# Moving SBUF operands of a three-block network to other byte offsets

## The reference

```python
x = first_block(x, c, positions, ...)    # 2 layers: swiglu, hybrid conv/MLA or NSA attention, swiglu
x = second_block(x, mem, ...)            # 2 layers: forgetting attention + feed-forward, conv + mixture of 8 experts
return third_block(x, mem, ...)          # pooled + MoBA attention, cross attention, conv feed-forward

def swiglu(h, w13, w2):
    a, b = jnp.split(h @ w13, 2, axis=-1)
    return (jax.nn.silu(a) * b) @ w2
```

## The kernel before, in words

| operand | address before | offset before |
|---|---|---|
| `hh`, `hl` | 24736, 32928 | 160 |
| `whi`, `wlo` | 86400, 119168 | 128 |
| `AR` | 179488 | 32 |
| `f_gh`, `f_gl` (float 224 of `AR` and on) | 180384 | 160 |
| `uh`, row k (float 3840 + 264 k) | 194848 + 1056 k | 32, 64, 96, 128, 160, 192, 224, 0 |
| `e_zeh`, `e_zel`, `e_gh`, `e_gl` | 182560 and on | 32 |

## Time and profile before

### The profile page before, as it was taken

The page is one execution under the profiler, slowest core; times in us unless marked ns, Lnnn a source line. Parts: engine busy times, 40 slices in busy tenths (PEclk is TensorE's granted clock), DMA queues, the critical chain, the costliest instruction groups (busy, mean ns, idle before and its releaser), DMA issues.

```text
span 3083.6 us, 48420 instructions
## 1 busy us (share of the span) xinstructions
PE 2999.6 (97%) x20659; PEld 2751.1 (89%) x20659; DVE 2343.1 (76%) x2704; ACT 1725.0 (56%) x1982; POOL 73.7 (2%) x143
## 2 busy tenths in 40 slices
PE   9999999999989999899989999999999999999999
PEld 8999899999979998899987888888888888899999
DVE  6887788888657566665777898898898898766675
ACT  5435443534535445444655777777777777555553
POOL 0110001010000000000000000000000000000000
PEclk9999999999999999999999999999999999999999
DMA  8785468587513543255415998998999899533353
GB/s 335 283 317 195 163 245 302 212 308 258 199 69 142 215 162 138 76 192 191 148 64 209 364 358 334 365 355 333 365 356 366 333 359 366 213 124 137 123 201 114
DMA packets 112381, 739.27 MB, mean 240 GB/s; under 512 B 12480, under 2 KB 12480, under 8 KB 32160
## 3 DMA queue, kind: packets, MB, share of 16 engines
q1 hardware_dynamic: 92304, 662.77, 57.3%
q0 software_dynamic: 19856, 73.34, 6.8%
HBM read 735.01 MB, written 1.05 MB: 239 GB/s over the span
## 4 chain that ended last, share of the span: by engine, by line
PE 86%; DVE 9%; ACT 3%; issue 1%; DMA 0%; SPq 0%; DVEq 0%; ACTq 0%
PE ps L560 65%; PE ps L559 19%; PE ps L569 2%; DVE wlo L2983 2%; ACT whi L1986 2%; DVE AF L2962 1%; DVE att L2971 1%; DVE T L2953 1%; DVE hl L2953 1%; DVE gf L2965 0%; ACT cv L1971 0%; DMA ring<-in_r 0%; DVE cv L2962 0%; DVE T L2962 0%; DVE AR L2962 0%
## 5 line engine op out<-in xcount | busy, mean ns | idle before, releaser
L2983 DVE TENSOR_TENSOR wlo<-ring,whi 128x2048 fp32r<-128x2048 f32 x620 | 1416.3, 2290 | 399.0 <-ACT whi L1986 398.3
L1986 ACT ACTIVATE whi<-ring 128x2048 fp32r<-128x2048 f32 x620 | 1184.4, 1914 | 310.6 <-issue 199.0
L560 PE MATMUL ps<-whi,AR 128*128 128x512 f32 (+1 forms) x2884 | 910.7, 392 | 0.3 <-DVE AF L2953 0.3
L560 PE MATMUL ps<-hh,whi 128*128 128x256 f32 x2272 | 641.8, 282 | 0.4 <-DVE hl L2953 0.4
L560 PEld LDWEIGHTS ps<-whi,AR 128*128 128x128 f32 x2884 | 535.5, 188 | 115.3 <-DVE AF L2953 0.7
L560 PE MATMUL ps<-hl,whi 128*128 128x256 f32 x2272 | 634.4, 279 | 0.0
L560 PE MATMUL ps<-hh,wlo 128*128 128x256 f32 x2272 | 634.3, 279 | 0.0
L560 PE MATMUL ps<-wlo,AR 128*128 128x512 f32 (+1 forms) x1442 | 557.4, 387 | 0.0
L560 PEld LDWEIGHTS ps<-hh,whi 128*128 128x128 f32 x2272 | 426.2, 188 | 5.8 <-issue 1.5
L560 PEld LDWEIGHTS ps<-hl,whi 128*128 128x128 f32 x2272 | 426.1, 188 | 1.2 <-issue 1.0
L560 PEld LDWEIGHTS ps<-hh,wlo 128*128 128x128 f32 x2272 | 425.9, 187 | 0.3
(11 more groups left out here) (275 smaller groups left out, 3481.6 us busy)
## 6 DMA issues: line engine op xcount, KB each, us to landing
ring<-in_w SPq DMA_DIRECT2D x620, 1024.0 KB, 4.9
rring<-in_r POOLq DMA_DIRECT2D x135, 512.0 KB, 5.0
first<-in_r SPq DMA_DIRECT2D x8, 512.0 KB, 18.4
ring<-in_r SPq DMA_DIRECT2D x4, 512.0 KB, 8.6
rring<-in_r SPq DMA_DIRECT2D x3, 512.0 KB, 17.4
AF<-in_mem SPq DMA_DIRECT2D x1, 1024.0 KB, 8.2
X<-in_x SPq DMA_DIRECT2D x1, 1024.0 KB, 16.2
AF<-in_cst POOLq DMA_DIRECT2D x1, 1024.0 KB, 5.3
```

The lines of the kernel that those rows point to most:

```text
L560: return self.e.matmul(out, l, r, start=start, stop=stop)
L1986: self.e.activation(N.whi[:, c % HB, :], N.ring[:, c % RING, :], ACT.Copy).then_inc(N.sem["hi"], 1)
L2983: self.e.tensor_tensor(N.wlo[:, c % HB, :], N.ring[:, c % RING, :], N.whi[:, c % HB, :].bitcast(F32), ALU.subtract).then_inc(N.sem["lo"], 1)
```

## The change

Nothing is added to or taken from the instructions, and the order on each engine stays: only the addresses change. `gain` and `ca` change places around `hh` and `hl`; a 192-byte tensor `gap` goes in ahead of `whi` and a 160-byte `gap2` ahead of `AR`; `f_gh`/`f_gl` move by 16 floats; the unshifted early halves get an arena of their own, `vh`/`vl`, with rows of 256 floats at float 3888 of `AR`. The shifted ones stay in `uh`/`ul`.

| operand | offset before | offset after |
|---|---|---|
| `hh`, `hl` | 160 | 64 |
| `whi`, `wlo` | 128 | 64 |
| `f_gh`, `f_gl` | 160 | 64 |
| unshifted early halves | 32, 64, ... 224, 0 by row | 64 in all rows |
| shifted early halves (258 columns) | 32, 64, ... 224, 0 by row | 128, 160, ... 64, 96 by row |
| `e_zeh`, `e_zel`, `e_gh`, `e_gl` | 32 | 128 |
| `AR` and the other pieces cut from its start | 32 | 128 |
| `ring`, `rring` | 128 | 128 |

```diff
         self.X = sb("X", [P, 8, S])
-        self.ca = sb("ca", [P, 8])
+        self.gain = sb("gain", [P, 2, 3, 8])
         self.hh = sb("hh", [P, 8, S], F32R)
         self.hl = sb("hl", [P, 8, S], F32R)
-        self.gain = sb("gain", [P, 2, 3, 8])
+        self.ca = sb("ca", [P, 8])
...
         self.rring = sb("rring", [P, RAW, CR])
+        self.gap = sb("gap", [P, 48])
...
         self.misci = sb("misci", [1, 8], I32)
+        self.gap2 = sb("gap2", [P, 40])
...
-        self.f_gh, self.f_gl = zip(*[pair(at) for at in (224, 736, 1248)])
+        self.f_gh, self.f_gl = zip(*[pair(at) for at in (240, 752, 1264)])
         ar.n = 3840
         self.uh, self.ul = ar.take(8, UP), ar.take(8, UP)
         assert ar.n <= self.AF.shape[1] - 8 * S
+        ar = Arena(self.AR)
+        ar.n = 3888
+        self.vh, self.vl = ar.take(8, S), ar.take(8, S)
+        assert ar.n <= self.AF.shape[1] - 8 * S
...
+def early_halves(net, key):
+
+    return (net.uh, net.ul) if EARLY[key][0] == "mod" else (net.vh, net.vl)
...
-                    t = self.mm3(b[j][:, 0:n], whi[:, o:o + P], wlo[:, o:o + P], N.uh[:, k, 0:n], N.ul[:, k, 0:n],
+                    t = self.mm3(b[j][:, 0:n], whi[:, o:o + P], wlo[:, o:o + P], uh[:, k, 0:n], ul[:, k, 0:n],
                                  k == 0, k == 7)
```

More of the change, by code:

```diff
@@ L746, in wide_early @@
         n = S + 2 if EARLY[h][0] == "mod" else S
+        uh, ul = early_halves(N, h)
         cs = [self.chunk(s) for s in specs]
@@ L2095, in early @@
         gain, shift = gain_of(N, which)
+        uh, _ = early_halves(N, key)
         if self.loaded:
@@ L2104, in early @@
                 self.ready_x(j)
-                self.act(N.uh[:, j, 0:S], N.X[:, j, :], ACT.Copy, (key, "uhi", j), scale=gain[:, j:j + 1])
+                self.act(uh[:, j, 0:S], N.X[:, j, :], ACT.Copy, (key, "uhi", j), scale=gain[:, j:j + 1])
             if k == 0 and shift is not None:
-                self.act(N.uh[:, :, S:S + 2], shift.unsqueeze(2).to_broadcast([P, 8, 2]), ACT.Copy, (key, "ush"))
+                self.act(uh[:, :, S:S + 2], shift.unsqueeze(2).to_broadcast([P, 8, 2]), ACT.Copy, (key, "ush"))
             self.act(N.T[:, k:k + 2, :], N.X[:, k:k + 2, :], ACT.Square, (key, "sq", k), (key, "sq", k + 1))
@@ L3147, in early_after @@
         gain, shift = gain_of(N, EARLY[key])
+        uh, ul = early_halves(N, key)
         def rest(k):
@@ L3151, in rest @@
                 self.wait_ge("act", (key, "ush"))
-                self.tt(N.ul[:, :, S:S + 2], shift.unsqueeze(2).to_broadcast([P, 8, 2]), N.uh[:, :, S:S + 2].bitcast(F32),
+                self.tt(ul[:, :, S:S + 2], shift.unsqueeze(2).to_broadcast([P, 8, 2]), uh[:, :, S:S + 2].bitcast(F32),
                         ALU.subtract)
             self.wait_ge("act", (key, "uhi", k))
-            self.stt(N.ul[:, k, 0:S], N.X[:, k, :], gain[:, k:k + 1], N.uh[:, k, 0:S].bitcast(F32), ALU.mult, ALU.subtract,
+            self.stt(ul[:, k, 0:S], N.X[:, k, :], gain[:, k:k + 1], uh[:, k, 0:S].bitcast(F32), ALU.mult, ALU.subtract,
                      (key, "un", k))
```

## The result

The changed kernel is slower: 3119.02 us, median of four runs (3114.74 to 3121.98), against 3088.96 for the kernel before (3084.6 to 3091.05). The ratio is 1.0097, with a 95% interval of 1.0083 to 1.0111, so it lost some 30 us. The prediction had 3015.

A forecast was written before the change was run, and what follows sets the result against it. TensorE's distance between matmul starts was taken to bound the kernel. Linears 35, early halves 1.6, weights moving 3 and experts 35 made 75 us off the 3083.6 span, 3009, plus 6.9: 3015 us, range 2985 to 3092.

The forecast's parts named there:

- offset 64, moving, with 128 stationary, is 3.4 ns faster: Early product row k = 1: 113.3 ns per 256-column matmul, against 116.7 at offset 160 in the linears.
- I take 3.33: Linears: 3.33 ns off each of 11,664 matmuls, 38.9 us, less 4 us for longer waits: 35 us.
- The bound that the same paragraph names: Linears: a loss of 3.3 ns each, 38.5 us, from the slowest steady pair in the trace, 120.0 ns.
- Experts: 4038 matmuls of 512 columns: 10 ns less each, 233.3 to 223.3, 40 us, of which 35 stay after DMA.
- The lower bound on record: Experts: no gain at all, if 512 columns behaved like 258, where the offset does not matter.
- Early halves and weights moving: Unshifted early halves gain 1.6 us on 336 matmuls; weights moving, some 670 matmuls, gain 3.9 us, of which 3 taken.
- Shifted early product: Early product with 258 columns, where the offset does not matter: no gain.
- What takes over: With TensorE faster, DMA is nearest, about 383 GB/s to be had: 5 us taken off the experts' 40.
- From span to time: The 6.9 us by which the median stands above the span, added to 3009 to give 3015.
- Slower: 64 against 64 over 116.7 ns in the linears, experts' gain absent: 3100 to 3128, middle 3115; chance 0.13.
- the pair rival: The pair of offsets counts: linears lose 19 to 38 us, experts gain 35; 3071 to 3096, middle 3083; chance 0.13.
- No-change: Row k = 1's pace came from its place in memory, not its offset; linears and experts keep pace: 3090; chance 0.10.

The follow-up runs named there:

- The maps: Two kernels of their own, 64 pairs of moving and stationary offset at 256 and 512 columns, in two orders: 1130.35 and 1130.97 us.
- the first map: Kernel of its own: 64 streams of 48 matmuls, one per pair of moving and stationary offset, in the first of two orders; 1130.35 us.
- `whi` at 128: The changed kernel with `whi` and `wlo` back at offset 128, all else at the changed offsets: 3062.92 us, ratio 0.9906.
- 64 bytes lower: The changed kernel, `whi` still at 64, with `hh`, `hl`, gated and unshifted halves at 0 and `AR` at 64: 3054.64 us, ratio 0.9896.
- the experts alone: The kernel before with `AR` moved from 32 to 128, gated halves kept at 160: 3077.05 us, ratio 0.9964.
- distance 112: The changed kernel with `whi` at 128, `AR` at 128 and the activation halves at 240: 3048.34 us, ratio 0.9885.

## Why the prediction was wrong

**The step that failed** is the first on which the sum stood, "offset 64, moving, with 128 stationary, is 3.4 ns faster", carried to 64 against 64. The term "I take 3.33, since it is the row with the moving operand where the change puts it" changed one thing too many: the change moved the stationary operand as well. The row belonged to distance 192, the change made distance 0, and there the linears run at 120.0 ns. The bound that the same paragraph names, 3.3 ns or 38.5 us the other way, is what came: in full stream 116.80 became 119.90 ns and 116.72 became 120.00, 26.4 + 10.5 = 36.9 us on 8505 and 3215 matmuls, of which 32.9 were measured. The 4 us between them are shorter pauses and fewer matmuls at half clock in the slower kernel, as many us as the prediction had taken off for longer ones in a faster. The maps, the kernel with only `whi` moved, and the one with `whi` put back all show it.

**The evidence was also thinner than it looked.** Rows k = 1 of two products at 113.3 ns seemed to be a repeated measurement. But the pair (64, 128) also runs at 117.8, in the first map and in over half of a kernel's linears, and at its distance the start of the stream decides. Two rows of 12 and 9 matmuls could not show that.

**Experts.** 40 us were taken for (64, 128) at 512 columns, from bounds taken at 256. At 512 columns that pair costs 233.4 ns, exactly what (128, 32) costs, so the term is 0.7 us the other way. The lower bound on record, "nothing at all", was the right end, but the reason was not that nothing depends on the distance at 512 columns: 0 is worth 5 ns there. The width changes which distance is good.

**Early halves and weights moving.** The early rows got slower with the rest (120.0 against 118.3). Weights moving against AR, 96 to 192, gained 1.0 us on 288 matmuls; against `hh` and `hl`, 224 to 0, 384 lost 0.3. 3 us gain were taken for both. Pieces at AR's start that move against `whi` (160 to 64) gained 0.8 on 336, where nothing was taken.

**Shifted early product.** Predicted unmoved, and it is. TensorE in time order in the changed kernel, k = 1 from its start to that of k = 2, 1.45 us for 12 or 120.8 ns as in the earlier trace rows:

```profile
381.55 0.41 PE L571 MATMUL ps<-AR,whi 128*128 128x258 f32 x2
...
383.00 0.40 PE L571 MATMUL ps<-AR,whi 128*128 128x258 f32 x2
```

**VectorE and ScalarE.** Predicted to keep their durations, though `whi` and `wlo` moved (`ring` stayed at 128); they do, against the earlier trace rows:

```profile
L2996 DVE TENSOR_TENSOR wlo<-ring,whi 128x2048 fp32r<-128x2048 f32 x620 | 1416.4, 2290 | 412.1 <-ACT whi L1998 411.3
L1998 ACT ACTIVATE whi<-ring 128x2048 fp32r<-128x2048 f32 x620 | 1183.6, 1913 | 327.3 <-issue 197.4
```

**What takes over.** DMA was named as nearest, 5 us of 40 taken off for it. In the changed kernel nothing was faster, so the term was not tested there. The four kernels with faster experts lost 3.6 (`whi` at 128), 2.0 (64 bytes lower), 4.8 (the experts alone) and 9.1 us (distance 112) of a gain of 20. So the term was right in kind, and 5 us lies inside what half the gain cost; for 40 it is likely too small, which no run tested. A part of the loss is the clock behind the pauses, which was no term of the sum. The bandwidth itself was judged well (364 GB/s at 0.96 is 379 at full use, where 383 was the estimate). A comparison of means does not show such a loss: the last kernel's stage has a mean share of only 0.93, and waits all the same:

```profile
1640.00:2640.00 1000.00, 991.51 (x4669) 821.35 (x4668) 880.15 (x658) 730.39 (x613) 1.06 (x2) 1.00 0.93 353
```

**From span to time.** The sum adds 6.9 us for what lies around the span. In every run on record with both figures the time is 1.7 to 1.9 us above the run's own span (3118.82 against 3117.0 for the changed kernel). The other 5 us were the difference between one execution and the median of others.

**The rivals.** "Slower" came true as written, 3115 in its middle, with the mechanism named (64 against 64 over 116.7 ns) and the experts' gain absent. It got a chance of 0.13. What should have raised it was in the rows: the only equal pair in the trace ran at 118.3, slower than the linears' 116.7, and the pair rival's counter-argument, "1.7 ns is small beside the 4 to 7 that the moving offset makes", compared rows in which the stationary offset stood still. With the moving offset varied against one stationary offset only, no row could separate the offset from the distance, and the two theories then deserved nearly equal chances. The Trainium skill (TensorE: Matmul & The Clock Gate, Step-by-step: what each phase is for) gives the two operands independent ports and lets a weight load take nothing from the running matmul; measured paces that hang on the distance between the two addresses do not agree with it as the whole story. No-change fell too. Its rule, 16-byte lines (the Trainium skill, SBUF — State Buffer, Door 1: The DMA port swizzle), would have all multiples of 16 alike; they run from 113.3 to 120.0 ns, and a distance that leaves 12 is often better.

**What stays open.** Why the distance matters, and what sets which rhythm a stream takes. The runs show on what the pace depends, the two addresses and the start of the stream; where on the chip the two streams meet, if they do, was not measured.

## What to carry to other kernels

When a trace offers a natural experiment on one operand's address, ask what stood still in it: here only the difference between two addresses could be read, and a change that moves both ends may leave it or undo it. In a kernel bound by short matmuls, a small map of pairs at the kernel's own widths (some 1.1 ms of chip time) is cheaper than an argument, and each width needs its own. Before a gain on the bounding engine is summed up, give the transfer that runs at over nine tenths its share of the stage.

## What the runs showed of the hardware that was not expected

- In a full stream of matmuls of 128 x 128 with 256 columns in fp32r, the distance from start to start runs from 113.3 to 124.5 ns, by the difference of the moving and the stationary address modulo 256; with 512 columns from 226.7 to 240.0 ns. For multiples of 32 all 64 pairs show it, for steps of 4 only a stationary operand at 128 was measured. The best difference seen is 112 or 192 at 256 columns and 0 at 512.
- Some differences have two steady rhythms, and one other matmul ahead of the stream decides between them: 192 has 113.3 and 117.8 ns, 32 has 116.7 and 117.8, 160 has 117.4 and 120.0 (between the pairs of one map). At 112 only 113.3 was seen once a stream had settled, which took up to 20 matmuls.
- A difference that leaves 4 over a multiple of 16 costs up to 6% at 512 columns (240.0 against 226.7 ns); those that leave 12 stay at or under 231.9.
- 258 columns keep about 120 ns (118.6 to 122.2 by row in three kernels, but for the very first row), whatever the row's offset, even where 256 columns ran at 113.3.
- Behind three pauses of TensorE in the experts, 2.2 to 3.1 us from start to start, the granted clock fell to half, and 7, 7 and 8 matmuls were 427 ns apart in place of 228. Such stretches cost 1.4 to 1.6 us each, a fourth pause, of 2.0 us, had none behind it.
